# A hybrid decoder layer: the transposes of the attention output move into the next pass of the attention loop, and the first output projection starts with its attention half

## The reference, cut to what matters

```python
def trunk_layer(x, pos, conv_prev, ffn_prev, attend, ...):
    xn = rms_norm(x, attn_norm_w)
    q, k, v, qi, ki, wi, cx, cb, cc, ga, gc = jnp.split(xn @ w_in, split_at, axis=-1)
    ...
    attn = attend(q, k, v, qi, wi, ki).reshape(B, T, ATTN_DIM)
    u_hist = jnp.concatenate([conv_prev.astype(x.dtype), cc * cx], axis=1)
    conv_out = cb * causal_dwconv(u_hist, conv_w)
    mixed = jax.nn.sigmoid(ga) * (attn @ w_o_attn) + jax.nn.sigmoid(gc) * (conv_out @ w_o_conv)
    h = x + mixed @ w_merge
    hn = rms_norm(h, ffn_norm_w)
    g, val = jnp.split(hn @ w_up, [D_FF], axis=-1)
    ...
    y = h + (jax.nn.silu(g_conv) * val) @ w_down
    return y, k, v, ki, conv_state, ffn_state
```

## Time and profile before

| | |
|---|---|
| time, median of 3 runs | 1806.97 us (1803.0 to 1807.43) |
| the profiled execution: its own time | 1806.21 us |
| the profiled execution: span of the trace | 1804.4 us |
| TensorE busy (matmuls) | 1741.4 us, 97% of the span |
| VectorE busy | 1081.8 us, 60% |
| GpSimd busy | 697.1 us, 39% |
| ScalarE busy | 593.9 us, 33% |
| mean granted clock of TensorE | 0.983 |

### The profile page before, as it was taken

The page is one execution under the profiler, slowest core; times in us unless marked ns, Lnnn a source line. Parts: engine busy times, 40 slices in busy tenths (PEclk is TensorE's granted clock), DMA queues, the critical chain, the costliest instruction groups (busy, mean ns, idle before and its releaser), DMA issues.

```text
span 1804.4 us, 29595 instructions
## 1 busy us (share of the span) xinstructions
PE 1741.4 (97%) x10989; PEld 1674.8 (93%) x10989; DVE 1081.8 (60%) x1798; ACT 593.9 (33%) x844; POOL 697.1 (39%) x349
## 2 busy tenths in 40 slices
PE   7999999999999899998999999999999999999998
PEld 5868899999999788887999999999999999999998
DVE  5579999998999555556442354444344344344344
ACT  5755642322112577775112231211211211112110
POOL 3405752554886466662122232322322223223220
PEclk9999999999999899999999999999999999999999
DMA  5321112113775323232333131111111111111102
GB/s 192 86 64 36 46 47 84 60 59 130 245 228 182 117 71 88 78 95 83 121 122 121 47 105 36 50 45 46 46 46 47 46 46 46 46 42 51 47 0 99
DMA packets 58513, 146.58 MB, mean 81 GB/s; under 512 B 14602, under 2 KB 14730, under 8 KB 58298
## 3 DMA queue, kind: packets, MB, share of 16 engines
q1 hardware_dynamic: 52642, 125.03, 22.0%
q10 hardware_dynamic: 5072, 16.22, 2.5%
q0 software_dynamic: 720, 4.29, 0.6%
HBM read 125.91 MB, written 19.71 MB: 81 GB/s over the span
## 4 chain that ended last, share of the span: by engine, by line
PE 58%; issue 15%; POOL 10%; DVE 9%; ACT 5%; SPq 2%; DMA 1%; ACTq 0%; DVEq 0%; POOLq 0%
PE PS L534 16%; PE PX L962 13%; PE PS L914 9%; PE PS L869 5%; POOL WLO L1459 4%; PE PS L822 3%; PE PS L792 2%; DVE S L1803 2%; POOL DLO L1625 2%; POOL TG L1621 2%; DVE M L1801 2%; PE PX L805 2%; PE PS L850 2%; DVE LD L1783 2%; PE PS L637 1%
## 5 line engine op out<-in xcount | busy, mean ns | idle before, releaser
L1459 POOL TENSOR_TENSOR WLO<-WRAW,WHI 128x1024 fp32r<-128x1024 f32 x102 | 256.6, 2515 | 527.7 <-ACT WHI L1004 527.5
L914 PE MATMUL PS<-X2H,WHI 128*128 128x344 f32 (+1 forms) x1032 | 330.4, 320 | 0.3 <-POOL WLO L1459 0.3
L914 PE MATMUL PS<-X2L,WHI 128*128 128x344 f32 (+1 forms) x1032 | 330.4, 320 | 0.0
L914 PE MATMUL PS<-X2H,WLO 128*128 128x344 f32 (+1 forms) x1032 | 330.0, 320 | 0.0
L534 PE MATMUL PS<-XH,WHI 128*128 128x346 f32 (+1 forms) x984 | 321.2, 326 | 6.0 <-POOL WLO L1459 4.8
L534 PE MATMUL PS<-XL,WHI 128*128 128x346 f32 (+1 forms) x984 | 317.9, 323 | 0.0
L534 PE MATMUL PS<-XH,WLO 128*128 128x346 f32 (+1 forms) x984 | 317.2, 322 | 0.0
L1803 DVE MATCH_REPLACE8 S<-M,S 128x1024 f32<-128x1024 f32 (+3 forms) x224 | 206.0, 926 | 0.0
L534 PEld LDWEIGHTS PS<-XH,WHI 128*128 128x128 f32 x984 | 186.3, 189 | 15.9 <-issue 9.2
L1801 DVE MAX8 M<-S 128x8 f32<-128x1024 f32 (+3 forms) x224 | 200.8, 932 | 0.4
L2005 DVE TENSOR_TENSOR HX<-HX,PX 128x344 f32<-128x344 f32 x264 | 135.3, 513 | 108.3 <-PE PX L962 108.3
(11 more groups left out here) (282 smaller groups left out, 3163.7 us busy)
## 6 DMA issues: line engine op xcount, KB each, us to landing
WRAW<-wtiles SPq DMA_DIRECT2D x93, 512.0 KB, 3.6
KR<-cache_k SPq DMA_DIRECT2D x64, 256.0 KB, 3.0
RING<-cache_v SPq DMA_DIRECT2D x64, 256.0 KB, 2.9
DRAW<-wdown SPq DMA_DIRECT2D x11, 1024.0 KB, 4.9
gates<-EV ACTq DMA_DIRECT2D x13, 519.0 KB, 3.8
WRAW<-wtiles ACTq DMA_DIRECT2D x10, 512.0 KB, 5.7
XT<-xT SPq DMA_DIRECT2D x8, 528.0 KB, 7.7
SGA<-gates SPq DMA_DIRECT2D x8, 519.0 KB, 3.5
```

Source lines behind the costliest of these rows:

```text
L914: last = nc.tensor.matmul(PS[b][:, c, 0:n], w[b][:, kk, :], x[:, kk, t0 + c * n:t0 + (c + 1) * n], start=(kk == 0 and p == 0), stop=(kk == ...
L1459: nc.gpsimd.tensor_tensor(WLO[b][:, :, :], WRAW[b][:, :, :], WHI[b][:, :, :].bitcast(F32), ALU.subtract).then_inc(w_lo[b], 1)
```

## The change

In passes 1 to 3, TensorE appends one transpose to `pv(u)` of every odd unit u: block t = u // 2 of the pair of heads that the pass before finished, from AT into `px_t`, columns 352 to 480 of the third bank of `PS[1]` (`turn_heads`). It is issued ahead of `a_pv`. ScalarE copies it to AH at the end of its step u (`heads_high`). VectorE, in `out` of an odd unit, waits for that copy (`at_h`) ahead of the scaled output, and raises `a_o` behind a subtraction that makes AL (`split_heads`). ScalarE and VectorE wait for `k_saved` ahead of pass 1, since AH overlays stored keys.

At the seam only the fourth pair of heads is left: nine transposes in three groups, two copies and two subtractions of 512 columns and one each of 16. The four matmuls on OD go to a corner of PX. The projection runs in the order attention chunks 0 and 1, convolution chunks 0 and 1, convolution chunk 2, attention chunk 2. ScalarE and VectorE take the wide AH and AL pieces ahead of COH and COL, the small ones behind the second of four COH tiles.

```diff
+        px_t = PS[1][:, 2, 352:352 + P]
+        at_last = ((PX[0], 0, 4), (PX[1], 4, 4), (PS[1][:, 2, 0:32], 8, 1))
...
+                if u % 2 == 1 and not (isinstance(i, int) and i == 0):
+                    last = turn_heads(u // 2, i - 1)
                 last.then_inc(a_pv, 1)
+
+            def turn_heads(t, j):
+
+                return nc.tensor.transpose(px_t[:, 0:ROWS[t]], AT[0:ROWS[t], t, ds(j * P, P)], CK[0:ROWS[t], C_ID:C_ID + ROWS[t]])
...
+            pe.wait_ge(at_l, 2)
+            pe.wait_ge(d_o, 2)
...
+            pe.wait_ge(w_lo[1], 22)
+            out_part(1, 0, 0, 2)
+            pe.wait_ge(co_l, 3)
+            pe.wait_ge(co_lp, 1)
+            out_part(1, 1, 0, 2)
+            pe.wait_ge(at_l, 4)
+            out_part(1, 1, 2, 3)
+            out_part(1, 0, 2, 3).then_inc(mm[1], 1)
...
+            def heads_high(t, i):
+
+                w = P if t < 8 else NMETA
+                act.wait_ge(a_pv, NU * i + 2 * t + 2 + FREE)
+                act.sem_inc(held, 1)
+                nc.scalar.copy(AH[:, ds(i - 1, 1), t * P:t * P + w].rearrange("p a t -> p (a t)"), px_t[:, 0:w]).then_inc(at_h, 1)
...
+                    if u % 2 == 1 and not (isinstance(i, int) and i == 0):
+                        heads_high(u // 2, i)
...
+            heads_last(0)
+            heads_last(1)
             for j in range(4):
                 act.wait_ge(co_in[j], 16)
                 nc.scalar.copy(COH[:, j, C0:T], CRAW[j][:, C0:T]).then_inc(co_h, 1)
...
+                if j == 1:
+                    heads_last(2)
+                    act.wait_ge(d_at, 1)
+                    nc.scalar.copy(AH[:, :, TPR:T], at_past.rearrange("p (j t) -> p j t", j=4)).then_inc(at_h, 1)
...
+                if u % 2 == 1 and not (isinstance(i, int) and i == 0):
+                    dve.sem_inc(held, 1)
+                    dve.wait_ge(at_h, NB * (i - 1) + u // 2 + 1)
+                    dve.sem_inc(held, 1)
                 ins = nc.vector.tensor_scalar(AT[0:r, b, ds(i * P + e * HD, HD)], px_out[u % 2][0:r, :],
                                               SM[0:r, 36 + u:37 + u], None, ALU.mult)
...
+                if u % 2 == 1 and not (isinstance(i, int) and i == 0):
+                    ins = split_heads(u // 2, i - 1)
                 ins.then_inc(a_o, 1)
+
+            def split_heads(t, j):
+
+                w = P if t < 8 else NMETA
+                high = AH[:, ds(j, 1), t * P:t * P + w].rearrange("p a t -> p (a t)")
+                low = AL[:, ds(j, 1), t * P:t * P + w].rearrange("p a t -> p (a t)")
+                return nc.vector.tensor_tensor(low, px_t[:, 0:w], high.bitcast(F32), ALU.subtract)
```

More of the change, by code:

```diff
@@ L232, in build @@
         px_out = [t[:, 2, 32:32 + HD] for t in PS]
-        at_banks = (PX[0], PX[1], PS[0][:, 0, :], PS[0][:, 2, :])
+        px_t = PS[1][:, 2, 352:352 + P]
+        at_last = ((PX[0], 0, 4), (PX[1], 4, 4), (PS[1][:, 2, 0:32], 8, 1))
+        at_past = PX[0][:, 0:32]
         px_dec = [t[:, 2, 96:352] for t in PS]
@@ L862, in _, with out_part @@
                 attend(i, i == 3, decode_values)
-            def out_part(b, q):
-                for c in range(NCH):
+            def out_part(b, q, c0=0, c1=NCH):
+                for c in range(c0, c1):
                     for kk in range(4):
@@ L881, in _ @@
             pe.wait_ge(a_o, 4 * NU + FREE)
[L882 to L886, removed]
+            for px, t0, nt in at_last:
+                for t in range(t0, t0 + nt):
+                    last = nc.tensor.transpose(px[:, (t - t0) * P:(t - t0) * P + ROWS[t]], AT[0:ROWS[t], t, 3 * P:4 * P],
                                                CK[0:ROWS[t], C_ID:C_ID + ROWS[t]])
                 last.then_inc(at_t, 1)
[L889 to L900, removed]
+            pe.wait_ge(at_l, 2)
+            pe.wait_ge(d_o, 2)
+            for j in range(4):
+                last = nc.tensor.matmul(at_past[:, 8 * j:8 * j + 8], OD[:, j * P:(j + 1) * P], CK[:, C_OH:C_OH + 8],
+                                        start=True, stop=True)
+            last.then_inc(d_at, 1)
+            pe.wait_ge(w_lo[1], 22)
[6 more added lines that the diff above has]
+            out_part(1, 0, 2, 3).then_inc(mm[1], 1)
             outs(0, 22, 1)
@@ L1368, in _ @@
             attend(0, False)
+            act.wait_ge(k_saved, 16)
             with act.Fori(1, 3) as i:
@@ L1377, in _, with heads_last @@
             act.wait_ge(v_saved, 32)
+            def heads_last(g):
+                px, t0, nt = at_last[g]
+                w = nt * P if nt > 1 else NMETA
+                act.wait_ge(at_t, g + 1)
+                nc.scalar.copy(AH[:, 3, t0 * P:t0 * P + w], px[:, 0:w]).then_inc(at_h, 1)
+            heads_last(0)
+            heads_last(1)
             for j in range(4):
@@ L1899, in _ @@
             attend(0, False)
+            dve.wait_ge(k_saved, 16)
             with dve.Fori(1, 3) as i:
@@ L1912, in _, with low_last @@
                                                op0=ALU.mult, op1=ALU.mult).then_inc(d_o, 1)
+            def low_last(g):
+                px, t0, nt = at_last[g]
+                w = nt * P if nt > 1 else NMETA
+                dve.wait_ge(at_h, 27 + g + 1)
+                nc.vector.tensor_tensor(AL[:, 3, t0 * P:t0 * P + w], px[:, 0:w], AH[:, 3, t0 * P:t0 * P + w].bitcast(F32),
+                                        ALU.subtract).then_inc(at_l, 1)
+            low_last(0)
+            low_last(1)
             for j in (0, 1, 3):
@@ L1916, in _ @@
                 nc.vector.tensor_tensor(COL[:, j, C0:T], CRAW[j][:, C0:T], COH[:, j, C0:T].bitcast(F32), ALU.subtract).then_inc(co_l, 1)
[L1917 to L1924, removed]
+                if j == 1:
+                    low_last(2)
+                    dve.wait_ge(at_h, 27 + 4)
+                    step(nc.vector.tensor_tensor(AL[:, :, TPR:T], at_past.rearrange("p (j t) -> p j t", j=4),
+                                                 AH[:, :, TPR:T].bitcast(F32), ALU.subtract))
+            dve.wait_ge(at_h, 27 + 5)
             nc.vector.tensor_copy(AL[:, :, T:TP], AH[:, :, T:TP].bitcast(F32)).then_inc(at_l, 1)
```

## The result

The changed kernel takes 1818.15 us in the median of four runs (1813.57 to 1818.49), the kernel before 1806.81 us in the runs beside it: a ratio of 1.0061, 95% interval 1.004 to 1.0083. The forecast was 1808.9 us, no measurable change, with a range up to 1816.0; the change is slower, and lies outside. The profiled execution is the shortest of the four, 1813.57 us, with a span of 1811.7.

What follows compares the result with a forecast made beforehand. TensorE was taken to set the pace in the attention loop, busy 50.9 of 54 us a pass. From 1806.2 us, 9.3 lost in the loop and 6.6 won at the seam gave 1808.9 us, range 1802.0 to 1816.0.

Steps and rivals of the forecast that it cites:

- The loop: Attention passes 1 to 3: added transposes and stalls lose 9.3 us, at least 3.2, at most 15.4.
- rival 1: Loop stalls are swallowed by slack in TensorE's queue: 1802.8 us, or 1801.6 with the better seam; chance 0.20.
- (a): Loop, TensorE: 27 added transposes at 0.12 us each in a stream cost 3.2 us.
- (b): Loop: unit 3's later output delays unit 7's QK matmuls by 0.6 us a pass, 1.8 us in all.
- (c): Loop, ScalarE's queue: the copy delays the exponential behind it, 2.7 us at unit 7's transposes, 0.6 us at unit 16.
- (d): Pass boundary: unit 17's hand-over lengthens the chain TensorE waits for by 0.5 us, at two boundaries 1.0 us.
- The units taken at nothing: Loop units 1, 7, 9, 11 and 15: hand-overs cost nothing, covered by ScalarE's 34.7 us of waiting for VectorE.
- The seam: Last unit to output projection: fewer transposes and attention chunks first win 6.6 us, bounds 4.7 to 7.8.
- Rival 2: Loop lockstep: ScalarE and VectorE stop at every odd unit, 27 x 0.75 = 20 us, 1822.8 us; chance 0.20.
- Rival 3: Seam: early attention half only waits before the convolution half, whose inputs start later; 1811.9 us; chance 0.05.
- the signs: Loop 6 to 12 us longer, seam 4 to 7 us shorter, waits grown at unit 7, last convolution subtraction over 3 us.

Runs made afterwards that it cites:

- e9: Kernel before plus, in passes 1 to 3, one ScalarE wait for unit 5's values and a copy of a constant; ratio 1.0074.
- e10: Changed kernel with transposes of units 3 and 5 hung on 2 and 6, and ScalarE's transpose copies for units 7 and 16 ahead of the exponential; ratio 0.997.
- e6: Changed kernel with the transposes of units 3, 5 and 17 hung on units 4, 6 and 10; ratio 1.0013.
- e7: Changed kernel with one of nine transposes moved, that of unit 5 to unit 6; ratio 1.0014.
- e11: As e10, with the last transpose hung on unit 16 in place of 17; ratio 0.9959, median 1801.43 us.
- e8: Changed kernel with ScalarE's transpose copies for units 7 and 16 put ahead of the next exponential; ratio 0.9964.

## Why the prediction was wrong, point by point

**What failed is a term that the sum did not have.** The loop was priced at full clock, 9.3 us, and at full clock it cost 8.6. The prediction knew that the granted clock falls at the seam, and used it there; in the loop it allowed for the clock only as luck on the fast side (rival 1). The waits that the loop gained let the clock fall: 5.4 to 7 us more in the two traces of the changed kernel, and e9 shows that one such wait does it without the rest of the change. With 5.4 to 7 us for it the sum is 1806.2 + 8.6 - 7.5 + 5.4 to 7 = 1812.7 to 1814.3, and the profiled execution took 1813.57. The median, 1818.15, is 4.6 us higher still; the lower mean clock of those runs accounts for it, though not where it fell. The range ended at 1816.0 because its upper side was made of longer stalls (and of a gain of 5.6 us at the seam, though the bound worked out for that was 4.7); the stalls came as forecast, and the clock had no term on that side. The trace of before had the sign: the full clock all through the loop but for three stretches, each just behind one of the three pass starts, where TensorE waited 1 to 1.8 us.

**(a) Transposes: right.** 27 x 0.12 = 3.2 forecast. At full clock the loop grew by 8.6 us, 6.1 of it idle time, which leaves 2.5; e10, which has hardly another loss, stands 3.0 over the kernel before. The other price, 275 ns for one (the Trainium skill, TensorE: Matmul & The Clock Gate, Part 4: PE-mode transpose), would have made 7.4 us by estimate. The trace agrees with that figure as the duration of one: the transpose at L834 above took 0.28 us. But it started 0.12 us behind a matmul that took 0.28 as well, so they overlap, and what one added to the loop was about 0.1 us.

**(b) Hand-over at unit 3: right.** The logits of unit 7 waited 0.80, 0.80 and 0.63 us, 2.2 in all; 1.8 forecast.

**(c) ScalarE's queue: right.** Unit 7: 1.05, 1.05 and 0.98 us against 0.17, 2.6 in all; 2.7 forecast. Unit 16: 0.47, 0.48 and 0.25 against 0.17, 0.7 in all; 0.6 forecast.

**(d) Pass boundary: right.** 2.23 and 1.33 us against 1.84 and 1.01, 0.7 in all; 1.0 forecast. Together (b) to (d) make 6.2 us against 6.1 forecast, and the idle time of the three passes grew by 6.1 in all. The units taken at nothing (1, 7, 9, 11, 15) show no stall.

**The seam: right, one step aside.** 6.6 forecast, 7.5 measured. VectorE's last convolution subtraction met GpSimd's, as forecast, but later in it: it stood still for 1.3 us and took 2.54, where "over 3" was to show it:

```profile
L1962 DVE TENSOR_TENSOR COL<-CRAW,COH x3: 1225/1228/2537, 854.2 to 858.5; 128x1038 fp32r<-128x1038 f32 x3
```

It ended at 861.0, and TensorE, which had begun the attention chunks at 856.06, came to the convolution half at 861.2; so that half cost no wait, where the sum had 0.8 us (846.3 to 847.1). That is nearly all of the 0.9 us by which the seam was better. The forecast's own terms without that wait give 846.3 + 8.0 = 854.3, 7.4 us won; the 7.8 of its bound starts the half at 845.9, when by the same sum TensorE was still at the attention chunks.

**The rivals.** Rival 1, the stalls swallowed, did not happen here; e10 is what it would have looked like, 0.3% faster. Rival 2, lockstep, had the right sign by the wrong mechanism: 27 hand-overs at 0.75 us would have added 20 us at full clock; 8.6 were added in all, and e6, e7 and e10 show that it depends on the place. Rival 3 fell with the seam. The chance of slower, 0.23, rested on lockstep; it should have rested on the clock. Of the signs, the stalls came at the places named; the loop's 14.0 us lies above the 6 to 12 and the seam's 7.5 above the 4 to 7.

**What stays open.** Why the clock stays down for 3 us behind one stall and for 13 behind another (e9, pass 2), why it falls behind 0.48 us at unit 16 and not behind 0.80 at unit 7's logits, and why e10 and e11 differ, no run here tells. That the clock falls behind these waits is shown by adding one wait (e9) and by taking it away (e8); how much it falls is only measured, case by case.

## What to carry to other kernels

Price a new wait on TensorE, where it sets the pace, twice: its own length, and a slow stretch that may stand behind it; in this kernel, 2.5 us of wait at one place became 12, while waits at another place cost their own length only. Which it is has to be measured, over several runs, since two executions of one kernel can differ by a slow stretch or two. Before hanging a copy into another engine's queue, look at what stands behind it there: work that the pace-setting engine is already waiting for must come first, and to turn two instructions round can be worth more than the whole change. A change that fails at one place may be good at the others, so find the place before undoing it.

## What the runs showed of the hardware

A wait of 1 us on TensorE, otherwise busy, was enough for the granted clock to fall from the 2.4 GHz level to 1.2 GHz behind it (e9: wait until 696.77, slow from 698 to 701). Other waits, of 0.54 to 0.80 us ahead of logits, had no such fall behind them. The Trainium skill tells of something near it (TensorE: Matmul & The Clock Gate, A second HAM failure mode: psum-queue depth-cycling): in one kernel, frequent short idle spells between groups of matmuls made the clock swing between its two levels. The traces here agree that short spells can do it; they need not be frequent, as e9 added one per pass.

A VectorE tensor_scalar of 128x128 from SBUF to SBUF, with one input, took 2.44 us beside a GpSimd operation of 2.45 us, and 0.20 to 0.22 where none ran beside it; the same operation reading PSUM took 163 to 283 ns in all 27 places:

```profile
L1895 DVE TENSOR_SCALAR AL<-PS x27: 163/280/283, 680.9 to 837.4; 128x128 f32 x16, 128x128 fp32r<-128x128 f32 x8, 128x16 f32 x2, 128x16 fp32r<-128x16 f32 x1
```

The prediction used the rule on two SBUF inputs (the Trainium skill, SBUF — State Buffer, Who interferes with whom); the same section says that a tensor_scalar can enter a mode that uses the port pair shared with GpSimd, with one input. This trace agrees.
